# Two plain units instead of four in the first feed-forward, its block sums made beside them

## The reference

```python
# first block
mod = silu(c) @ w_ada + b_ada             # six rows of 1024: sh1, sc1, gt1, sh2, sc2, gt2
x = x + gt1 * (mixed @ w_out)             # attention, pooling and convolution make mixed
h = rmsnorm(x, g_ffn) * (1 + sc2) + sh2
gate, up = split(h @ w_gate_up)           # 1024 -> 2 x 2816
x = x + gt2 * ((silu(gate) * up) @ w_down)
x = rmsnorm(x, g_final)
# second block
h = h + 0.5 * swiglu(rms_norm(h, ffn1_norm), w_gate, w_up, w_down)     # again 2816 wide
...                                       # two attentions, merged by gates
h = h + merged @ w_out
h = h + 0.5 * swiglu(rms_norm(h, ffn2_norm), w_gate, w_up, w_down)
return rms_norm(h, final_norm)
```

## Time and profile before

| | |
|---|---|
| median of 3 runs | 1675.16 us (1674.34 to 1675.46) |
| profiled execution, its own time | 1675.03 us |
| its span in the trace | 1673.2 us |
| granted TensorE clock, mean of the span | 0.995 |
| busy: TensorE, weight loads | 99%, 86% |
| busy: VectorE, ScalarE, GpSimd | 66%, 46%, 11% |

### The profile page before, as it was taken

The page is one execution under the profiler, slowest core; times in us unless marked ns, Lnnn a source line. Parts: engine busy times, 40 slices in busy tenths (PEclk is TensorE's granted clock), DMA queues, the critical chain, the costliest instruction groups (busy, mean ns, idle before and its releaser), DMA issues.

```text
span 1673.2 us, 26140 instructions
## 1 busy us (share of the span) xinstructions
PE 1649.6 (99%) x10265; PEld 1435.6 (86%) x10265; DVE 1107.1 (66%) x1664; ACT 774.3 (46%) x1292; POOL 191.9 (11%) x193
## 2 busy tenths in 40 slices
PE   7999999999999999999999999999999999999998
PEld 5777688889989989989899887777887899998997
DVE  4888856466757776767768526765555777586773
ACT  3565644223525565524345423554543554253553
POOL 0110210011022011010110231011000200101102
PEclk9999999999999999999999999999999999999999
DMA  9733137357388577464764155222237865537721
GB/s 335 245 127 125 43 105 218 113 148 174 101 216 211 141 164 190 133 145 124 207 159 117 38 144 111 63 59 66 76 100 184 210 161 141 149 80 199 178 87 51
DMA packets 287646, 235.79 MB, mean 141 GB/s; under 512 B 16524, under 2 KB 272456, under 8 KB 287512
## 3 DMA queue, kind: packets, MB, share of 16 engines
q1 hardware_dynamic: 250416, 185.10, 35.4%
q0 software_dynamic: 36752, 48.95, 16.4%
q10 hardware_dynamic: 360, 0.13, 0.0%
HBM read 226.28 MB, written 6.36 MB: 139 GB/s over the span
## 4 chain that ended last, share of the span: by engine, by line
PE 86%; DVE 7%; ACT 3%; DMA 2%; issue 1%; DVEq 0%; ACTq 0%
PE psum L730 15%; PE psum L732 15%; PE psum L731 15%; PE psum L1085 12%; PE psum L1088 11%; PE psum L1087 11%; PE psum L1235 1%; PE psum L1200 1%; PE psum L1255 1%; DVE ring_lo L2277 1%; DMA w_raw<-in_w_in 1%; DMA w_raw<-in_w_out 1%; DVE w_lo L2037 1%; PE psum L936 1%; PE psum L896 1%
## 5 line engine op out<-in xcount | busy, mean ns | idle before, releaser
L2277 DVE TENSOR_TENSOR ring_lo<-part_raw,ring_hi 128x1024 fp32r<-128x1024 f32 (+1 forms) x291 | 349.0, 1200 | 168.9 <-ACT ring_hi L1688 168.0
L1688 ACT ACTIVATE ring_hi<-part_raw 128x1024 fp32r<-128x1024 f32 (+1 forms) x291 | 300.5, 1037 | 313.3 <-PE psum L732 211.7
L1085 PE MATMUL psum<-h_hi,ring_hi 128*128 128x256 f32 x928 | 263.6, 284 | 0.0
L1087 PE MATMUL psum<-h_lo,ring_hi 128*128 128x256 f32 x928 | 263.3, 284 | 0.0
L1088 PE MATMUL psum<-h_hi,ring_lo 128*128 128x256 f32 x928 | 263.3, 284 | 0.0
L730 PE MATMUL psum<-hid_hi,ring_hi 128*128 128x512 f32 (+1 forms) x536 | 207.3, 387 | 0.5 <-DVE x_res L2548 0.5
L731 PE MATMUL psum<-hid_lo,ring_hi 128*128 128x512 f32 (+1 forms) x536 | 206.9, 386 | 0.0
L732 PE MATMUL psum<-hid_hi,ring_lo 128*128 128x512 f32 (+1 forms) x536 | 206.8, 386 | 0.0
L1085 PE MATMUL psum<-n_hi,ring_hi 128*128 128x256 f32 x696 | 197.6, 284 | 1.5 <-DVE n_lo L2516 0.8
L1087 PE MATMUL psum<-n_lo,ring_hi 128*128 128x256 f32 x696 | 196.9, 283 | 0.0
L1088 PE MATMUL psum<-n_hi,ring_lo 128*128 128x256 f32 x696 | 196.9, 283 | 0.0
(11 more groups left out here) (333 smaller groups left out, 2833.5 us busy)
## 6 DMA issues: line engine op xcount, KB each, us to landing
part_raw<-in_ffn_w_up SPq DMA_DIRECT2D x66, 512.0 KB, 5.0
part_raw<-in_w_gate_up SPq DMA_DIRECT2D x51, 512.0 KB, 5.7
w_raw<-in_w_in SPq DMA_DIRECT2D x50, 512.0 KB, 3.8
part_raw<-in_ffn_w_gate SPq DMA_DIRECT2D x44, 512.0 KB, 6.4
part_raw<-in_ffn_w_down SPq DMA_DIRECT2D x32, 512.0 KB, 5.0
part_raw<-in_ffn_w_gate POOLq DMA_DIRECT2D x22, 512.0 KB, 7.9
part_raw<-in_ffn_w_up POOLq DMA_DIRECT2D x22, 512.0 KB, 9.8
sq<-in_w_ada SPq DMA_DIRECT2D x20, 512.0 KB, 4.6
```

The lines of the kernel that those rows point to most:

```text
L1085: pe.matmul(o, a_hi, b_hi, start=fresh, stop=False, skip_group_check=True)
L1087: pe.matmul(o, a_hi, b_lo, start=False, stop=False, skip_group_check=True)
L1688: act.activation(ring_hi[slot][:, 0:n], pool_raw[s_][b][:, 0:n], ACT.Identity).then_inc(f_high, 1)
L2277: dve.tensor_tensor(ring_lo[slot][:, 0:n], raw_[:, 0:n], ring_hi[slot][:, 0:n].bitcast(F32), ALU.subtract).then_inc(f_ready, 1)
```

## The change

`PLAIN` becomes 2, so units 2 and 3 of feed-forward 0 turn into block units in round 0; round 0's `downs` now follow unit 3. The four sums of h move from the `downs` to the four plain column tiles, one behind each, through one scratch tile. Two modulation rows instead of one are used behind each tile. ScalarE's high part of sum 0 to 2 stands in the next tile's step, and that of the last sum behind the last tile, since it overwrites a block of h that plain products read. TensorE waits for three finished sums before T1 of unit 2, and for the fourth before T3. GpSimd issues the accumulating transfers of unit 2 between modulation rows 1 and 2. `mod_columns` keeps its place in the `downs` of round 0, `mod_group` goes right before them. In stage `out2` the five transfers of unit 0 are split: two behind slab 3, three behind slab 4.

```diff
-        temps = [place(f"temp{n}", [P, KQ, TQ], F32, T_AT + n * CHUNK) for n in range(2)]
+        temp = place("temp", [P, KQ, TQ], F32, T_AT)
...
-        PLAIN = ROUNDS[0][1]
+        PLAIN = 2
         KM = KU - PLAIN
+        SUMS_AT = (0, 1, 2, 3)
+        ROWS_AT = ((0, 1), (2, 3), (4, 5), (6, 7))
...
# TensorE, first_ffn and unit
-                downs(0, 0, lambda: mod_columns(GT2 // KD))
-                for r in range(1, len(ROUNDS)):
+                for r in range(len(ROUNDS)):
                     for u in units_of(r):
-                        unit(0, u, None, None)
-                    downs(0, r)
+                        if u >= PLAIN:
+                            unit(0, u, None, None)
+                    downs(0, r, (lambda: mod_columns(GT2 // KD)) if r == 0 else None)
...
                 if f == 0 and u == PLAIN:
-                    pe.wait_ge(q_ready, KQ)
+                    pe.wait_ge(q_ready, KQ - 1)
                 await_item(("T1", f, u))
...
                 pe.wait_ge(run_copied, 3 * m - 1)
+                if f == 0 and u == PLAIN:
+                    pe.wait_ge(q_ready, KQ)
                 product(y, "T3", R3, f, u).then_inc(f_prod, 1)
...
# SyncE, stage out2
-                if i == 2:
+                if i == 3:
                     sp.wait_ge(w_used, S_OUT2)
                     sp.wait_ge(m_ready, KD)
-                    pair_parts(0, *(w.rearrange("(k p) n -> p k n", p=P) for w in weights2[:2]), 2)
+                    gate2, up2 = (w.rearrange("(k p) n -> p k n", p=P)[:, :, 0:2 * P] for w in weights2[:2])
+                    fetch(("B12", 2, 0), up2[:, 0:KQ, :], 2 * P)
+                    fetch(("B11", 2, 0), gate2[:, 0:KQ, :], 2 * P)
+                if i == 4:
+                    fetch(("B12+", 2, 0), up2[:, 0:KQ, :], 2 * P)
+                    fetch(("B22", 2, 0), up2[:, KQ:KD, :], 2 * P)
+                    fetch(("B21", 2, 0), gate2[:, KQ:KD, :], 2 * P)
...
# ScalarE, sums_high, first_ffn and unit
+                if q == KQ - 1:
+                    act.wait_ge(f_prod, prod["up", 0, 2 * PLAIN - 1])
+                act.activation(dst, temp[:, :, :], ACT.Identity).then_inc(q_high, 1)
...
                     high_after("up", 0, n)
+                    if n - 1 in SUMS_AT[:KQ - 1]:
+                        sums_high(n - 1)
                     act.wait_ge(hid_set, n + 1)
                     act.activation(hid_hi[:, n, :], t_hid[:, :], ACT.Identity).then_inc(hid_high, 1)
-                downs(0, 0, lambda i, n: sums_high(i) if i < KQ else None)
-                for r in range(1, len(ROUNDS)):
+                sums_high(KQ - 1)
+                for r in range(len(ROUNDS)):
...
                 elif m == 1:
-                    act.wait_ge(q_ready, KQ)
+                    act.wait_ge(hid_ready, 2 * PLAIN)
                     act.wait_ge(mod_added, len(MOD_ORDER) * KD)
...
# VectorE, h_sum and first_ffn
+            def h_sum(q):
...
+                if q in (0, KQ - 1):
+                    one, two = (a22_hi, a22_lo) if q == 0 else (a11_hi, a11_lo)
+                    done(dve.tensor_tensor(temp[:, :, :], one.bitcast(F32), a21_hi.bitcast(F32), ALU.subtract))
+                    done(plus(two, ALU.add))
+                    plus(a21_lo, ALU.subtract).then_inc(combos_set, 1)
+                else:
+                    hi, lo = (a11_hi, a11_lo) if q == 1 else (a12_hi, a12_lo)
+                    done(less_both(hi))
+                    plus(lo, ALU.subtract).then_inc(combos_set, 1)
...
                     low_after("up", 0, n)
-                    if n < KD - 1:
-                        mod_step(3 * KD + n)
-                    if n == KD - 2:
-                        mod_step(3 * KD + n + 1)
+                    for r in ROWS_AT[n]:
+                        mod_step(3 * KD + r)
                     dve.wait_ge(hid_set, n + 1)
                     dve.wait_ge(hid_high, n + 1)
                     dve.tensor_tensor(hid_lo[:, n, :], t_hid[:, :], hid_hi[:, n, :].bitcast(F32), ALU.subtract)\
                        .then_inc(hid_ready, 1)
-                before_down()
-                downs(0, 0, down)
-                for r in range(1, len(ROUNDS)):
+                    if n - 1 in SUMS_AT[:KQ - 1]:
+                        sums_low(n - 1)
+                        dve.wait_ge(q_ready, n)
+                    if n in SUMS_AT:
+                        h_sum(SUMS_AT.index(n))
+                sums_low(KQ - 1)
+                for r in range(len(ROUNDS)):
                     for u in units_of(r):
-                        unit(0, u, r, None, None)
+                        if u >= PLAIN:
+                            unit(0, u, r, None, None)
+                    if r == 0:
+                        before_down()
                     downs(0, r, down)
...
-                if r == 0:
-                    h_sums(i)
...
# GpSimd
-            wait_filled(pool, ("mod", GT2 // KD))
             pool.wait_ge(rpb_copied, 16)
...
+            wait_filled(pool, ("sum", "ffn0"))
+            for r in range(3 * KD, 4 * KD):
+                pool.wait_ge(mod_added, r - 1)
+                mod_row(pool, r)
+                if r == 3 * KD + 1:
+                    add_weights(0, PLAIN, *weights0)
             for u in range(PLAIN, KU):
-                add_weights(0, u, *weights0)
+                if u > PLAIN:
+                    add_weights(0, u, *weights0)
```

More of the change, by code:

```diff
@@ L1785, in unit @@
             def unit(f, u, r, scales):
-                m, first, last = pair_count[f, u], u == ROUNDS[r][0], u == ROUNDS[r][1] - 1
+                m, last = pair_count[f, u], u == ROUNDS[r][1] - 1
+                first = u == ROUNDS[r][0] or m == 1
                 k = 2 * (u - ROUNDS[r][0])
@@ L2335, in sums_low @@
                 hi, lo = operand((N1, R2, N4, R3)[q])
-                dve.tensor_tensor(lo, temps[q % 2][:, :, :], hi.bitcast(F32), ALU.subtract).then_inc(q_ready, 1)
-            def plus(t, v, op):
-                return dve.tensor_tensor(temps[t][:, :, :], temps[t][:, :, :], v.bitcast(F32), op)
-            def less_both(t, v):
-                return dve.scalar_tensor_tensor(out=temps[t][:, :, :], in0=temps[1 - t][:, :, :], scalar=-1.0, in1=v.bitcast(F32),
-                                                op0=ALU.mult, op1=ALU.subtract)
@@ L2462, in unit @@
             def unit(f, u, r, scale_cols, scales):
-                first, last = u == ROUNDS[r][0], u == ROUNDS[r][1] - 1
+                first, last = u == ROUNDS[r][0] or pair_count[f, u] == 1, u == ROUNDS[r][1] - 1
                 k = 2 * (u - ROUNDS[r][0])
@@ L2839, in _ @@
                 pool.wait_ge(summed, SUM0 + n + 1)
-            wait_filled(pool, ("sum", "ffn0"))
-            for r in range(3 * KD, 4 * KD):
-                pool.wait_ge(mod_added, r - 1)
-                mod_row(pool, r)
             def add_weights(f, u, w_gate, w_up):
```

37 lines of the change are left out of this document (9 added, 28 removed).

## The result

The changed kernel takes 1684.48 us, median of 5 runs (1682.36 to 1686.88), beside 1675.04 of the kernel before (1674.34 to 1675.46): ratio 1.0051, 95% interval 1.0038 to 1.0064. The forecast was 1677.4, its range ended at 1681.5. The profiled executions have spans of 1682.7 and 1673.2, so the two traces hold the whole difference.

The account below looks back on a forecast made before the run. The prediction took TensorE, busy 99% of the span, as the bound: matmuls plus gaps in feeding it. Its terms, -3.2 - 0.9 + 7.9 - 2.8 + 1.3 = +2.3 on 1675.03, plus 0.1, gave 1677.4 us, range 1672.5 to 1681.5.

Parts of the forecast that it names:

- matmuls: Units 2 and 3 of feed-forward 0: a block unit takes 20.17 us, a plain one 21.76; two units give -3.2 us.
- the sums: Sums of h beside four plain tiles: VectorE runs late, T1 starts at 314.3, T2 ends at 322.6, not 314.7: +7.9 us.
- the predicted releaser: Before T1 of unit 2: a TensorE gap of some 5 us, ended by VectorE's low part of a sum.
- The remark that the low clock costs nothing: At unit 2: T1 at half speed would end about 319.0, still before ScalarE's copy at 319.7, so no loss.
- the downs: Round 0's downs: TensorE's wait for VectorE at 384.50 goes once the sums of h have left: -0.9 us.
- the ring: Behind feed-forward 1: six more items shift slots, `down1` waits for the last product, TensorE starts at 964.6: +1.3 us.
- the modulation rows: Beside the plain tiles: rows land 3.8 to 6.6 us after issue, needed after 8 to 9 us; no delay taken.
- The rival at 0.15: A modulation row lands late: at 11.3 us, rows 3, 5 and 7 add about 4 us, 1681.4; chance 0.15.
- stage out2: Stage out2 with the transfers split: slab 4 in time, slab 5's split earlier, gain 0.9 to 3.5 us; taken as -2.8.
- 1288.8 to 1292.0: Stage out2: predicted landing of slab 5, so that VectorE's split of it starts at 1290.5 to 1293.1.
- a gain of 0.4 more: Stage out2: if slab 5 shares engines with the second accumulating transfer, the gain is 3.2 us instead of 2.8.
- the wait moves on to slab 5: Rival in out2: it gives back only 0.9 us or less, a clock drop remains, 1679.3 to 1681; chance 0.12.

Follow-up runs that it names:

- experiment 12: Changed kernel run again twice: 1682.60 and 1684.18 us; kernel before with only out2's transfers split, run again twice: 1677.57 and 1678.35 us.
- experiment 8: Changed kernel with out2's five transfers together again and the last two modulation rows over 8 columns instead of 1024: 1679.63 us (1.0021).
- experiment 10: Changed kernel with out2's five transfers together again, three plain units and the modulation rows spread over six tiles: 1676.13 us (1.0003).
- experiment 7: Kernel before with one edit: `down1` waits for the last product of the middle feed-forward's last round: 1678.53 us (1.0016).
- Experiment 4: Kernel before with out2's transfers split and the two accumulating transfers of feed-forward 2's unit 0 cut to a quarter of their bytes: 1671.67 us (0.9974).
- experiment 3: Kernel before with out2's transfers split, the last three behind slab 5 instead of slab 4: 1671.70 us (0.9969); a second time 1671.90 (0.9977).
- experiment 6: Changed kernel with one line changed, out2's last three transfers behind slab 5 instead of slab 4: 1679.05 us (1.0017).
- experiment 9: Changed kernel, out2's transfers together, TensorE waiting for one sum before T1, the third before T2, ScalarE's first-product copy before the fourth sum's high part: 1682.71 us (1.0036).
- experiment 1: Kernel before with only out2's five transfers split, two at slab 3 and three at slab 4: 1677.68 us (1.0012).
- experiment 2: Changed kernel with out2's five transfers together again behind slab 2: 1682.57 us (1.0040).

## Why the prediction was wrong

**Right: what bounds the kernel, and the method of counting queues.** TensorE's offset moved only where a queue or a transfer made it wait, or where the granted clock differed.

**Right: matmuls and the sums, -3.2 and +7.9.** Measured together +5.0 against +4.7 (5.7 in the first repeat of experiment 12, with the late rows, and 5.1 in the second). T1 came 0.1 us from its predicted place, ended by the predicted releaser; experiments 8 and 10 show cause and cure (2.1 us less queue, T1 earlier by as much; 10 us more room, no wait). The remark that the low clock costs nothing held with no room to spare: T1 took 5.4 us instead of 2.9 and T2 began at 320.94, when ScalarE's copy had ended at 320.80.

**Right: the downs, -0.9** (measured -0.8), **and the ring, +1.3** (measured +1.3, and again alone in experiment 7).

**Partly right: the modulation rows.** The forecast took no delay, with landings of at most 6.6 us. In the changed kernel rows 2 and 3 landed 9.3 and 10.1 us after issue, right behind unit 2's second accumulating transfer, which GpSimd had issued 0.8 us ahead of row 2 and which took 8.8 us itself (8.9 to 11.2 us for these rows in all seven executions with two plain units). In the first execution VectorE waited only 0.5 us, at 288.38, in a place where it had that time; that nothing came of it was luck, since in the first repeat 0.7 us did. The rival at 0.15 came true in part: these two rows only (rows 4 to 7 took 3.8 to 5.4 us), and 0.7 to 1.0 us of T1 instead of 4. Whether they waited in GpSimd's queue or shared with the transfer, no run separates.

**Wrong: stage out2, -2.8.** The failed step is the landing of slab 5, "1288.8 to 1292.0", and the sentence that the second accumulating transfer "starts only when slab 5 is nearly through". In the kernel with the split alone, the cleanest to compare, slab 5 was issued at 1282.47 and the second accumulating one 1.4 us behind, so they ran side by side for 10 us, and slab 5 landed at 1294.43; less the 1.35 us by which that execution entered the stage late, 1293.1. That is 1.1 us past the upper bound, and 3 past 1290.1, which the -2.8 stands for. All six executions with the split lie past the bound, at 1292.6 to 1295.2. I had put all transfers on one line, a plain one at 1.4 to 1.8 us and an accumulating one at some 3. Experiment 4 shows why the line was wrong: with the accumulating transfers at a quarter of their bytes, the slab lands in at most 5.9 instead of 12.0 us. Slab 4's 13.47 us had the same company; that it had the same cause is inferred, since the unsplit order was not run with smaller accumulating transfers. The prediction had named both things behind it, the queue and the company, but priced the first. By the section on queues, rings and completion order of the Trainium skill's page DMA: Bandwidth & Descriptors, such transfers share each engine. The prediction weighed that as worth a gain of 0.4 more; the traces agree with the sharing, but as a loss: the second accumulating transfer, issued 1.4 us behind slab 5, landed after 10.4 us, within 0.2 us of the slab.

By experiment 12 the step is worth about +1.8, so it was off by 4.6: 3.4 of it up to T1, where the six executions average +0.6, because slab 5 was late (without that, experiments 3 and 4, the stage gains 3.2, close to the 2.8 forecast), and 1.2 by the low clock behind T1 that five of the six had. The rival "the wait moves on to slab 5" named this mechanism, at 0.12, but gave the stage back 0.9 "only or less"; its upper end, 1681, leaves room for a loss of 0.8 in the stage, and 1.8 was lost.

**The first 1.3 us are chance.** The stretch ahead of 258 us is the same code in all kernels here. One product in it starts at 195.8 us in the kernel before and in experiments 6, 8 and 9, at 197.7 to 198.1 in the first execution of the changed kernel and in experiments 1, 2 and 3, without relation to the edits. These four have a granted clock of 0.50 to 0.52 in 194.70 to 198.10, the kernel before and the changed kernel's repeats have 1.00 there; in the repeats the offset at the stretch's end is 0.2 and 0.6. Why the low clock falls there in some executions, no run shows. The prediction had rightly no term for it.

**The sum.** 1.3 + 5.0 - 0.8 + 1.3 + 0.3 + 2.3 = 9.4 of the profiled difference of 9.5. Over the three profiled executions the spans are 1682.7, 1681.0 and 1681.4, so 8.5 on average over the kernel before's 1673.2: 0.7 ahead of 261 us, 6.1 from there to out2's first product (5.8 to 6.4; the forecast's terms for it are +5.1), 1.8 in out2. With out2 at +1.8 in place of -2.8 the sum of the prediction is +6.9, 1682.0, just above its range. The wrong sign in out2 is 4.6 of the 7.1 us by which the median missed.

## What to carry to other kernels

Before moving transfers away from one that lands late, ask what made it late: its place in the queue or what ran beside it. If it was company, the move hands the same 11 to 14 us to the next transfer, and it pays only if the company moves too (here by one line, from +1.6 to -4.0 us by the medians). A queue counted instruction by instruction from single rows predicts to 0.1 us where an engine never waits; a landing time from a line of equal transfers does not. And an engine that was late as a whole was not helped by finer waits: the lateness came out at the next wait, with the clock's loss on top.

## What the runs showed of the hardware

- A plain transfer of 512 KB with two accumulating ones of 512 KB under way together beside it, and other plain ones around, landed in 11.4 to 14.1 us, in thirteen executions; in the order of experiment 1, with the accumulating ones at a quarter of their bytes, in 5.9. Two modulation rows issued right behind an accumulating transfer took 8.9 to 11.2 us, where the kernel before's rows took 3.8 to 6.6.
- The low clock behind a gap is worth its place: 0.50 granted in 315.50 to 319.80 us cost nothing in the changed kernel, since T1 had to wait for a copy, while in experiment 9 a mean of 0.66 in 321.00 to 328.50 took back 2.2 us of the 2.7 that the kernel led by at B21.
- One kernel's time varied by 7 us (1673.75 to 1680.98) in 35 runs beside the experiments, and by 1.1 in the 5 beside the first. Differences under 2 us needed the offsets of the timelines, and the granted clock at each place where they change.
